# The experts' first layer with no tile in plain fp32: every early tile by three rounded passes

## The reference, cut to what matters

```
q = (xb @ w_q).reshape(t, 8, 2, 128)
s = einsum('thpd,hpkd->thpk', q, sub_keys)              # scores of 128 keys
top_s, top_i = top_k(s, 16)
cand_s = top_s[:, :, 0, :, None] + top_s[:, :, 1, None, :]
best_s, best_pos = top_k(cand_s.reshape(t, 8, 256), 16) # 16 experts of 16384 per head
gate = softmax(best_s)
h = gelu(einsum('thkd,td->thk', u_table[idx], xb))      # the first layer
y = einsum('thkd,td' with gate * h and v_table[idx])    # the second layer
```

## Time and profile before

| engine | busy us | share of the span | instructions |
|---|---|---|---|
| PE | 1681.0 | 97% | 12718 |
| PEld | 1498.1 | 87% | 12718 |
| DVE | 1143.9 | 66% | 1883 |
| ACT | 789.0 | 46% | 1239 |
| POOL | 357.0 | 21% | 325 |

### The profile page before, as it was taken

The page is one execution under the profiler, slowest core; times in us unless marked ns, Lnnn a source line. Parts: engine busy times, 40 slices in busy tenths (PEclk is TensorE's granted clock), DMA queues, the critical chain, the costliest instruction groups (busy, mean ns, idle before and its releaser), DMA issues.

```text
span 1725.6 us, 32733 instructions
## 1 busy us (share of the span) xinstructions
PE 1681.0 (97%) x12718; PEld 1498.1 (87%) x12718; DVE 1143.9 (66%) x1883; ACT 789.0 (46%) x1239; POOL 357.0 (21%) x325
## 2 busy tenths in 40 slices
PE   6999999999999999999899999999999999999997
PEld 2999869977999889878779999999999988888886
DVE  4877857687555556874663899488899644444445
ACT  4433445656444454642243544555444433333334
POOL 2000100111000100000010667500000155555553
PEclk9999999999999999999999999999999999999999
DMA  9878855427555544430045455555555566666665
GB/s 361 292 268 304 307 209 192 147 98 265 186 202 183 191 143 147 149 126 21 27 171 173 123 173 177 164 159 159 160 160 160 173 193 194 194 192 189 193 193 169
DMA packets 64960, 314.40 MB, mean 182 GB/s; under 512 B 7216, under 2 KB 7632, under 8 KB 45776
## 3 DMA queue, kind: packets, MB, share of 16 engines
q1 hardware_dynamic: 63504, 305.94, 53.8%
q10 hardware_dynamic: 1280, 6.82, 1.1%
q0 software_dynamic: 64, 0.04, 0.0%
HBM read 311.72 MB, written 1.05 MB: 181 GB/s over the span
## 4 chain that ended last, share of the span: by engine, by line
PE 90%; DVE 3%; DMA 3%; ACT 2%; POOL 1%; issue 1%; SPq 0%; DVEq 0%; ACTq 0%
PE bank L421 25%; PE bank L422 25%; PE bank L423 25%; DMA ring<-in_stream 2%; PE bank L2904 2%; DMA ring<-in_experts 1%; PE bank L2877 1%; PE bank L2463 1%; POOL ring_rounded L3210 1%; DVE ring_rounded L381 1%; PE bank L1446 1%; PE bank L2476 1%; PE bank L855 1%; PE bank L2116 1%; PE bank L2130 0%
## 5 line engine op out<-in xcount | busy, mean ns | idle before, releaser
L423 PE MATMUL bank<-yb_rounded,ring_rounded 128*128 128x256 f32 x2032 | 575.0, 283 | 0.0
L2995 ACT CAST ring_rounded<-ring 128x1024 fp32r<-128x1024 f32 x248 | 260.5, 1051 | 291.8 <-DMA ring<-in_experts 291.8
L423 PEld LDWEIGHTS bank<-yb_rounded,ring_rounded 128*128 128x128 f32 x2032 | 389.6, 192 | 0.0
L381 DVE TENSOR_TENSOR ring_rounded<-ring,arena_rounded 128x1024 fp32r<-128x1024 f32 x230 | 272.8, 1229 | 110.0 <-ACT arena_rounded L367 109.3
L421 PE MATMUL bank<-yb_rounded,arena_rounded 128*128 128x256 f32 x1104 | 315.6, 286 | 1.2 <-issue 0.9
L422 PE MATMUL bank<-yT_rounded,arena_rounded 128*128 128x256 f32 x1104 | 312.8, 283 | 0.0
L3170 DVE TENSOR_TENSOR ring_rounded<-ring,ring_rounded 128x1024 fp32r<-128x1024 f32 x128 | 157.2, 1228 | 191.8 <-ACT ring_rounded L2995 191.8
L421 PE MATMUL bank<-yb_rounded,ring_rounded 128*128 128x256 f32 x960 | 278.4, 290 | 1.6 <-POOL ring_rounded L3210 0.7
L422 PE MATMUL bank<-yT_rounded,ring_rounded 128*128 128x256 f32 x960 | 271.4, 283 | 0.0
L367 ACT CAST arena_rounded<-ring 128x1024 fp32r<-128x1024 f32 x230 | 229.1, 1048 | 89.9 <-PE bank L421 77.8
L422 PE MATMUL bank<-ring_rounded,arena_rounded 128*128 128x512 f32 x688 | 268.1, 390 | 0.0
(11 more groups left out here) (447 smaller groups left out, 2611.7 us busy)
## 6 DMA issues: line engine op xcount, KB each, us to landing
ring<-in_stream SPq DMA_DIRECT2D x140, 1024.0 KB, 4.9
ring<-in_experts SPq DMA_DIRECT2D x256, 512.0 KB, 3.6
field<-in_stream SPq DMA_DIRECT2D x28, 512.0 KB, 7.1
field<-in_stream SPq DMA_DIRECT2D x4, 1024.0 KB, 8.4
yT<-in_stream SPq DMA_DIRECT2D x4, 512.0 KB, 5.9
field<-in_gains ACTq DMA_DIRECT2D x3, 512.0 KB, 7.8
field<-in_gains ACTq DMA_DIRECT2D x1, 1536.0 KB, 6.5
const<-in_const SPq DMA_DIRECT2D x1, 1473.0 KB, 11.7
```

The source lines that it names most:

```text
L381: ins = nc.vector.tensor_tensor(ring_r[:, g % SLOTS, half], ring[:, g % SLOTS, half], top.bitcast(F32), ALU.subtract)
L423: return first, pe.matmul(bank, s_rest, m_top, start=False, stop=stop)
L2995: nc.scalar.copy(expert_top[:, n % E_SLOTS, :], expert_w[:, n % E_SLOTS, :]).then_inc(expert_top_ready, 1)
```

## The change

All eight plain tiles become ordinary tiles of three rounded passes. `x_turned`, its 16 transposes on PE and its four copies on ACT go. ACT makes eight more tops and POOL eight more rests, and the counts of the semaphores follow.

```diff
-PLAIN = (6, 15, 17, 20, 30, 38, 41, 44)
@@ def split_no(tile):
-            return tile + 1 - len([p for p in PLAIN if p < tile])
+            return tile + 1
@@ def peer_pe(pe):
-            for t in range(TT):
-                for k in range(0, KT, 4):
-                    bank = A.take(pe)
-                    for j in range(4):
-                        ins = pe.transpose(bank[:, j * P:(j + 1) * P], xh[:, t, (k + j) * P:(k + j + 1) * P], ident)
-                    ins.then_inc(A.done, 1)
-            def plain_tile(tile): ...
             for tile in range(EARLY):
-                if tile == PLAIN[0]:
-                    A.evacuated_but(pe, 4)
-                if tile in PLAIN:
-                    plain_tile(tile)
-                else:
-                    u_tile(tile)
+                u_tile(tile)
@@ def top_expert():
-                if tops.term is None and n in PLAIN:
-                    tops.n += 1
-                    return
@@ def peer_act(act):
-            for t in range(TT):
-                for k in range(0, KT, 4):
-                    bank = A.get(act)
-                    nc.scalar.copy(x_turned[:, t, k:k + 4, :], bank[:, :].rearrange("p (j s) -> p j s", j=4)
-                                   ).then_inc(A.free, 1)
@@ def v_rests(g, j):
-                dve.wait_ge(expert_top_ready, mixed.at(NKEY - len(PLAIN) + mixed.n))
+                dve.wait_ge(expert_top_ready, mixed.at(NKEY + mixed.n))
@@ def peer_pool(pool):
             for tile in range(POOL_TILES):
-                if tile not in PLAIN:
-                    u_rest(tile)
+                u_rest(tile)
```

More of the change, by code:

```diff
@@ L2787, in program @@
         denom = take(TT * PH).rearrange("p (t h) -> p t h", t=TT)
-        x_turned = hidden[:, EARLY + 6:EARLY + 14, :].rearrange("p j s -> p (j s)").rearrange("p (t k s) -> p t k s", t=TT, s=P)
         pick_weights = field[:, HID:HID + S]
@@ L2860, in peer_pe @@
                     ins.then_inc(A.done, 1)
-            for t in range(TT):
-                for k in range(0, KT, 4):
-                    bank = A.take(pe)
-                    for j in range(4):
-                        ins = pe.transpose(bank[:, j * P:(j + 1) * P], xh[:, t, (k + j) * P:(k + j + 1) * P], ident)
-                    ins.then_inc(A.done, 1)
-            mixed = Count()
[L2870 to L2881, removed]
+            mixed = Count()
             def u_tile(tile):
```

## The result

The changed kernel takes 1732.7 us (median of 7, 1731.8 to 1734.2) against 1726.2 us before. The ratio is 1.0037, with a 95% interval of 1.0027 to 1.0047: slower by 6.5 us, 4.7 to 8.1 us by the interval. In two later jobs the same kernel, beside the one before, gave 1.0040 (1.0027 to 1.0053) and 1.0039 (1.0024 to 1.0053), both +7.5 us. The forecast was +4.0 us. The profiled execution took 1733.5 us, with a span of 1729.4 us.

The account below looks back on a forecast made before the run. PE, with 90% of the chain, was taken to bound the kernel. Terms of -6.35, +12.2 and -2.0 us gave +3.9, taken as +4.0: 1726.5 + 4.0 = 1730.5 us, range 1726.5 to 1735.5.

Parts of the forecast that it names:

- the third rival: DVE's picking finishes after ACT reaches the exponential, holding the tops behind it; 1732 to 1736 us, chance 0.17.
- ACT idle ahead of L3044 for more than 2 us: Sign that the forecast is wrong: ACT waits at the exponential because DVE's picking is late.
- What goes from PE: On PE, 16 transposes (1.75 us) and 0.57 us on each of eight plain tiles go, together 6.35 us.
- The quarter by the count of passes: On PE's plain tiles, three passes for four would save 0.86 us of 3.45; the forecast used 0.57 instead.
- The exclusion and its order: POOL's rests and DVE's steps exclude each other for a whole instruction, and alternate when both are queued.
- DVE first at a hand-off: Assumption that DVE goes before POOL when both are queued as an instruction ends.
- the recurrence: POOL's and DVE's queues carried forward from 956.8 us, rest by rest and step by step, with durations from the profile.
- The stalls: PE waits for POOL's rests at ten early tiles, 12.2 us together where there were 2.0.
- The picking: DVE's best_ready comes at 1101.1 us, before ACT reaches the exponential at 1103.4, so it adds no loss.
- The margin given: At the exponential, DVE's best_ready stays 2.3 us ahead of ACT, left of 11.7.
- POOL keeping up: POOL's rests do not stall PE, which wins 6.35 us less 0 to 2; about 1721 us, chance 0.10.
- The cancelling case: Only five or six of the ten PE waits come, offsetting PE's gain; 1724 to 1729.9 us, chance 0.25.

Follow-up runs that it names:

- the two versions through PSUM: The kernel before and the changed kernel, each with the picking's one-hot and small operands moved from SBUF to PSUM: 1724.8 us and 1718.9 us.
- late_exp: The changed kernel with ACT's exponential placed behind tile 46's gelu and tile 49's top instead of ahead of them: 1729.9 us, ratio 1.0024.
- psum_after: The changed kernel with the picking's one-hot and small operands moved to PSUM, each wide operation split into four: 1718.9 us, ratio 0.9959.
- half_plain: The kernel before with only its first four plain tiles (6, 15, 17, 20), the other four by three passes: 1729.9 us, ratio 1.0016.

## Why the prediction was right, and where its steps were off

The direction held, and so did the mechanism of the stalls. The size did not come as forecast: +6.5 us, and +7.5 in both later jobs, lie above the forecast's +3.3 to +5.5 and in the band of the third rival, +5.5 to +10, which had 0.17. Its sign came too: "ACT idle ahead of L3044 for more than 2 us" stood under "wrong", and ACT was idle for 2.85 us. That 1732.7 us still lies in 1726.5 to 1735.5 is owed to the range taking in part of that rival; a second mechanism came on top of the one that the sum had.

- **What goes from PE.** The turn: 1.75 us given, tile 0 comes 1.92 us earlier (6.58 to 4.66). The tiles: 8 x 0.57 us, and every undisturbed tile of the kernel after is 2.88 us. Between the two versions through PSUM 5.9 of the 6.35 us arrive. Right. The quarter by the count of passes would have been 6.9 us for the tiles alone, more than turn and tiles brought together.
- **The exclusion and its order.** The exclusion was right, and the carrying step of the forecast. L3054 takes 4.37 us (before: 4.32), and rests and DVE operations alternate wherever both are queued. "DVE first at a hand-off", put into the recurrence, was wrong for a short step behind another DVE step, as told under the picking.
- **The stalls.** Given 12.2 us at ten tiles, measured 10.4 at nine up to tile 45, plus a tenth of about 1.5 us at tile 46: 11.9. (The tenth was reckoned before tile 45 in the forecast, so to the end of tile 45 the sum was +3.9 and the trace has +2.0.) The list given was tiles 10, 17, 18, 21, 22, 33, 40, 41, 44, 45; measured 10, 17, 18, 21, 22, 34, 41, 42, 45, 46. The second half slipped by one tile; the likely reason is that the first half of the picking ended 2.2 us later than in the recurrence, by its L3093. Sizes are within 0.3 us of those given.
- **The picking.** This is the term that was mis-sized. `best_ready` was given at 146.1 us of the stage (1101.1) and came at 150.6. Nearly all of the 4.5 us between is L3093 (L3059 after): 2.45 us in place of 0.29, twice. The forecast did not name it among the steps that come near 2.3 us: with DVE first at a hand-off it slips in behind L3092 before POOL's queued rest. In the trace the queued rest goes first there, and each DVE step in a row waits for one. The margin given, 2.3 us, was in truth a wait of 2.8 us on ACT. The third rival, picking as bound, is thus what happened on top of the forecast's stalls. In the first profile's stage it is worth 1.4 us (4.9 less the -1.9 - 4.6 + 8.5 + 1.5 of the turn, the tiles and the stalls), and by `late_exp` 2.5 to 3.5 us in the medians, with the clock in it.
- **The clock.** Not in the sum at all: 1.5 us in two of three profiles, which were also the two whose time is their kernel's median to within 0.1 us. The text named no cost for a longer gap on PE; in the kernel before the largest stall of this stage was 0.7 us and the clock 1.00.
- **The rivals.** POOL keeping up would have needed rests of 2.4 us in the places of the wide steps; `psum_after` shows that case, at 1718.9 us. The cancelling case is about what `half_plain` is in size, 1729.9 us.
- **Chances.** Slower 0.62 came true, with the interval's lower end, 0.27%, above the 0.2% line; but the case to which most of it was given, +3.3 to +5.5 us, is not the one that came.

## What to carry to other kernels

Before work is moved to an engine that is 20% busy, look at what it shares with its neighbour in that stretch and add up both: POOL's 52 rests and DVE's two-input steps fit the time only while either had breaks. A chain of steps beside a saturated partner can pay the partner's whole instruction at each step, even for a step of 0.2 us, and the chain may be the next bound. Where two engines exclude each other over SBUF, try to keep one operand of the wide steps in PSUM: here it turned a loss of 6.5 us into a gain of 7, for some 5 us more of work on an engine that had the time.

## What the runs showed of the hardware

- DVE with two inputs in SBUF, and its casts, copies and shifts within SBUF down to 128 x 8 numbers, wait for a POOL subtraction of 2.4 us to end (0.23 us became 2.3), and two-input operations of 2.29 us hold it (four rests of 9.6 us took 13.6). With an operand or the result in PSUM neither waits (1.90 us for three operations beside a rest of 2.40 us; the shift with its result in PSUM took 0.29 to 0.30 us at all four places). The sum over 128 x 2048 and a rest run side by side: in the kernel before L3090 took 2.29 us from 1008.03, and the rest beside it 2.37 us from 1008.08.
- At a hand-off with both queued the engines take turns: two short DVE steps in a row took 2.3 us each beside a run of rests without a break.
- After a gap of 1.28 us on PE, 6.0 us of work and a gap of 2.36 us, the granted clock was 0.71 over 6 us, with matmul steps of the 1.2 GHz level, in two profiles; after 1.29 us, 8.9 us of work and 1.65 us, in three others, it stayed at 1.00.
